# A delta-rule inverse on other PSUM banks, ScalarE's bank copies ahead of its exponentials, and query-key products between the levels

## The chip, the cores and the metric

The kernel runs on one core of a Trainium2 chip, as one launch. The metric is the device time of that launch in microseconds. A core has five engines with a queue each: TensorE (PE) multiplies matrices and writes into PSUM (8 banks of 512 fp32 columns on 128 partitions), VectorE (DVE), ScalarE (ACT) and GpSimd (POOL) work elementwise, and SyncE (SP) issues DMAs. Each queue runs in order; queues wait for each other by named counters (semaphores).

## What is computed

Two transformer blocks over 16 meta tokens and 256 tokens of 1024 features. The change touches the gated delta rule of the first block only (4 heads, chunks of 64 tokens):

```python
decay = jnp.cumsum(g.reshape(b, h, n, c), axis=-1)
diff = decay[..., :, None] - decay[..., None, :]
lmask = jnp.where(causal, jnp.exp(jnp.where(causal, diff, 0.0)), 0.0)
a = jnp.where(strict, jnp.einsum("bhnid,bhnjd->bhnij", k_beta, k) * lmask, 0.0)
m = a + jnp.eye(c, dtype=a.dtype)
u = lax.linalg.triangular_solve(m, v_beta, left_side=True, lower=True, unit_diagonal=True)
...
qk = jnp.where(causal, jnp.einsum("bhnid,bhnjd->bhnij", q, k) * lmask, 0.0)
...
v_new = uc - jnp.einsum("bhcd,bhde->bhce", wc, state)
o = jnp.einsum("bhcd,bhde->bhce", qd, state) + jnp.einsum("bhij,bhje->bhie", qkc, v_new)
```

`dn_z` (`zs` in the kernel) gates the output through a SiLU, and `sb_qkv`'s values (`sbv`) belong to the other attention branch of the same block.

## The kernel before

The program is written out by hand, engine by engine; nothing reorders it. The block's stages follow each other: normalisation and transposes; the input projection `x @ w_in` in units of 512 columns; the delta rule; gates, attention branch and output projection; the experts; then the whole second block.

**Projection.** Units 1 to 6 are split into a high and a low part, so that a result is three products. Each result takes the next of the banks 0 to 3 in turn (`group[0]`); before result n, `bank_free(n)` waits until ScalarE has copied out result n-4 (counter `proj_out` at n-3 or more). Results 0 to 19 are the feature groups, then come 20 and 21 (attention values of the two token tiles, `sbv`), 22 (values of the meta tokens), 23 and 24 (`zs` of the two tiles). Between them TensorE computes column sums of squares into `SSQ_BANK` (banks 2, 3, 6, 7; L835), and transposes of decay and beta rows (L845, L852) into banks 4, 6 and 7.

**ScalarE's order there.** First eight logarithms of the sums (L1655), then eight exponentials (L1658), three small exponentials for the decays (L1660 to L1662), three large ones of the decay masks (L1665, which wait for VectorE's L2128), and only then the copies of results 20, 21 and 22 and the two SiLUs of 23 and 24 (L1670).

**The inverse.** For 9 matrices (`PARTS`: two parts of four for the tiles, one with the meta tokens) the inverse of I + A is built on blocks that double in size, level 0 to 5, in both 64-row halves at once, and joined at the end. `AT` is the transposed A, `XIc` the inverse and `XITc` its transpose. A level is: TensorE forms A X (`AX_BANK`, L893); VectorE masks it into `TMc` (L2161); TensorE forms the products for both forms (`ROW_BANK` L904, `XAX_BANK` L908); VectorE subtracts them (L2171, L2172). Level 0 needs no second product: VectorE sets X to I minus the mask (L2166), and GpSimd makes the transpose of that from `AT` with a constant of its own (`level0T`; L660 and L663). The query-key products stand in banks 0 and 1; VectorE multiplies them by the decay masks into `QKT` (L2154), ahead of level 0, since `AX_BANK` takes the same banks. So TensorE's wait ahead of level 0 (L884) is for all eight steps of VectorE's counter `chunk_dve`.

**Counters:** `proj` results done, `proj_out` results copied out, `ssq_psum`/`ssq_ln` column sums and their logarithms, `row_psum` transposed rows, `decay_rows` the operands of the decay masks, `chunk_psum` and `chunk_dve` products and VectorE's steps ahead of the inverse, `inv_ax`, `inv_masked`, `inv_xax`, `inv_step` the steps of a level, `stacked` GpSimd's steps.

Of the kernel before, what the change touches and what calls it, by code (L numbers as in the profile page):

```python
# [13 lines left out]
ALU = mybir.AluOpType  # L14
# [3 lines left out]
P = 128  # L18
# [3 lines left out]
NT = SEQ // P  # L22
# [42 lines left out]
HALVES = ["eye2", "level0T"] + [f"level{i}" for i in range(LEVELS - 1)]  # L65
# [11 lines left out]
def shape_constants():  # L77
# [17 lines left out]
    put["level0T"] = (q % 2 == 1) & (row == q - 1)  # L95
# [16 lines left out]
def build(nc, t):  # L112
# [422 lines left out]
    AX_BANK = B[0], B[1], B[6][:, 0:HW]  # L535
    ROW_BANK = B[2], B[3], B[6][:, HW:2 * HW]
    XAX_BANK = B[4], B[5], B[6][:, 2 * HW:3 * HW]
# [80 lines left out]
    def _(pool):  # L618
# [36 lines left out]
        for i, part in enumerate(PARTS):  # L655
            n = part.stop - part.start
            pool.wait_ge(S("chunk_dve"), 4 + i)
            pool.wait_ge(S("stacked"), 2 * i + 2)
            for rs in HALF_ROWS:
                last = nc.gpsimd.tensor_tensor(XITc[rs, part, :], AT[rs, part, rs], halves("level0T", n)[rs], ALU.mult)  # L660
            last.then_inc(S("stacked"), 1)
            pool.wait_ge(S("stacked"), 2 * i + 3)
            nc.gpsimd.tensor_tensor(XITc[:, part, :], halves("eye2", n), XITc[:, part, :], ALU.subtract).then_inc(S("stacked"), 1)  # L663
# [21 lines left out]
    def _(pe):  # L685
# [198 lines left out]
        pe.wait_ge(S("chunk_dve"), 8)  # L884
        pe.wait_ge(S("chunk_act"), 3)
        for lv in range(INNER):
            for i, part in enumerate(level_parts(lv)):
                if lv:
                    pe.wait_ge(S("inv_step"), inverse_count(lv - 1, i))
# [7 lines left out]
            for i, part in enumerate(level_parts(lv)):  # L897
                pe.wait_ge(S("inv_masked"), inverse_count(lv, i))
                if lv == 1:
                    pe.wait_ge(S("stacked"), 2 * i + 4)  # L900
# [671 lines left out]
    def _(sc):  # L1572
# [79 lines left out]

        for c in range(8):
            sc.wait_ge(S("ssq_psum"), c + 1)
            act(sq[:, c, :], SSQ_BANK[c % 4][:, 0:L], ACT.Ln, bias=C("eps6")).then_inc(S("ssq_ln"), 1)  # L1655
        for c in range(8):
            sc.wait_ge(S("ssq_ln"), c + 1)
            act(sq[:, c, :], sq[:, c, :], ACT.Exp, scale=-0.5).then_inc(S("rnorm"), 1)  # L1658
        sc.wait_ge(S("dec_out"), 1)
# [7 lines left out]
        for n, (dst, r, f) in enumerate([(sbv[:, 0, :], P, ACT.Copy), (sbv[:, 1, :], P, ACT.Copy), (sbv[:, 2, 0:P], P, ACT.Copy),  # L1667
                                         (zs[:, 0, :], P, ACT.Silu), (zs[:, 1, :], P, ACT.Silu)]):
            sc.wait_ge(S("proj"), N_FM + n + 1)
            act(dst, B[(N_FM + n) % 4][0:r, 0:dst.shape[1]], f).then_inc(S("proj_out"), 1)  # L1670
# [323 lines left out]
    def _(dve):  # L1994
# [157 lines left out]
        for i in range(NT):  # L2152
            dve.wait_ge(S("chunk_psum"), i + 9)
# [668 lines left out]
```

## Time and profile before

| | us |
|---|---|
| median of 3 runs | 1001.61 |
| lowest and highest | 1001.59, 1003.16 |
| the profiled execution | 1003.22 |
| its span in the trace | 1001.4 |
| TensorE busy in the span | 939.9 |
| VectorE busy | 572.1 |
| ScalarE busy | 389.2 |
| GpSimd busy | 37.9 |

The profiled execution has 1.8 us outside its span and is 1.6 us above the median. In a timeline each row is a merged group of instructions: its start, the time from the first start to the last end, engine, line, operation, output and input tiles, shapes and count; the brackets give idle time of the engine just before and what ended it. An fp32 product shows as two matmul records, and ends of matmuls are modelled, so neighbouring groups overlap by a tenth of a microsecond. DVE is VectorE, ACT ScalarE, POOL GpSimd, SPq the queue that issues DMAs.

### The profile page before, as it was taken

Reading aid. Unit: us, or ns where it says so; the run is one execution under the profiler, and the core shown is the slowest. Engines: PE = TensorE matmul, PEld = TensorE weight load, DVE = VectorE, ACT = ScalarE, POOL = GpSimd, SP = SyncE. Lnnn points to the kernel's source line nnn. Section 1 sums busy time; section 2 is a strip of 40 time slices with the busy share of each in tenths; the row PEclk is TensorE's granted clock in tenths of the full one; section 3 lists DMA queues with packets and bytes.
Section 4 is the critical chain, followed back from the end, with each engine's and each line's share of the span. In section 5 each row is a group of like instructions: output and inputs, shape, how many; then the busy total and the mean of one; then the engine's idle time right before and its main releaser. Section 6 shows DMA issues by size and latency. Waiting matters only on the chain.

```text
span 1001.4 us, 14260 instructions
## 1 busy us (share of the span) xinstructions
PE 939.9 (94%) x5875; PEld 730.4 (73%) x5875; DVE 572.1 (57%) x903; ACT 389.2 (39%) x525; POOL 37.9 (4%) x59
## 2 busy tenths in 40 slices
PE   8999889999998999388889999999999999999997
PEld 7998786777775434142568888888888898888885
DVE  5886474995673102010086567665566786666564
ACT  4556403773251111010166455433433454433341
POOL 1410120002000000000000000000000000000000
PEclk9999999999999999798999999999999999999999
DMA  9843420446699999999987523554554444554421
GB/s 324 254 169 109 163 92 1 168 169 259 245 366 386 419 421 419 419 420 419 382 319 250 182 85 115 188 202 168 179 213 153 168 169 171 207 211 168 169 82 43
DMA packets 67563, 226.35 MB, mean 226 GB/s; under 512 B 4128, under 2 KB 5440, under 8 KB 55856
## 3 DMA queue, kind: packets, MB, share of 16 engines
q1 hardware_dynamic: 65648, 220.21, 58.2%
q0 software_dynamic: 1632, 5.26, 1.7%
q8 instruction: 41, 0.67, 0.3%
q14 instruction: 18, 0.15, 0.1%
q10 hardware_dynamic: 224, 0.07, 0.0%
HBM read 224.47 MB, written 1.05 MB: 225 GB/s over the span
## 4 chain that ended last, share of the span: by engine, by line
PE 76%; DMA 9%; DVE 9%; ACT 3%; issue 2%; SPq 1%; ACTq 0%; DVEq 0%
PE bank L1511 16%; PE bank L1500 11%; PE bank L1501 6%; PE bank L1217 5%; PE bank L762 5%; DMA arena<-in_expert_w_up 4%; PE bank L1365 4%; DMA ring<-in_expert_w_up 3%; PE bank L775 2%; PE bank L1085 2%; PE bank L1127 2%; PE bank L1427 2%; PE bank L1369 2%; PE bank L807 1%; PE bank L1355 1%
## 5 line engine op out<-in xcount | busy, mean ns | idle before, releaser
L2607 DVE TENSOR_TENSOR w_lo<-ring,w_hi 128x2048 fp32r<-128x2048 f32 x76 | 170.5, 2287 | 76.4 <-ACT w_hi L1853 76.2
L1853 ACT ACTIVATE w_hi<-ring 128x2048 fp32r<-128x2048 f32 x76 | 141.4, 1915 | 95.0 <-PE bank L1511 86.3
L1500 PE MATMUL bank<-xT_lo_hi,w_hi 128*128 128x512 f32 x480 | 170.0, 398 | 0.0
L1501 PE MATMUL bank<-xT_lo_hi,w_lo 128*128 128x256 f32 x480 | 134.8, 281 | 0.0
L1500 PEld LDWEIGHTS bank<-xT_lo_hi,w_hi 128*128 128x128 f32 x480 | 90.2, 188 | 22.3
L1511 PE MATMUL bank<-w_hi,hidden_hi 128*128 128x512 f32 x256 | 100.0, 391 | 0.0
L1511 PE MATMUL bank<-w_hi,hidden_lo 128*128 128x512 f32 x256 | 99.8, 390 | 0.0
L1511 PE MATMUL bank<-w_lo,hidden_hi 128*128 128x512 f32 x256 | 99.7, 389 | 0.0
L1501 PEld LDWEIGHTS bank<-xT_lo_hi,w_lo 128*128 128x128 f32 x480 | 90.7, 189 | 0.5
L1217 PE MATMUL bank<-ring,arena 128*32 128x512 f32 x256 | 52.5, 621 | 20.5 <-DMA arena<-in_expert_w_up 20.5
L1951 ACT ACTIVATE arena<-bank 128x256 f32<-128x256 f32 x64 | 21.1, 382 | 109.9 <-PE bank L1501 106.1
L1511 PEld LDWEIGHTS bank<-w_hi,hidden_lo 128*128 128x128 f32 x256 | 48.0, 188 | 10.4
L1511 PEld LDWEIGHTS bank<-w_hi,hidden_hi 128*128 128x128 f32 x256 | 48.0, 188 | 10.2
L1511 PEld LDWEIGHTS bank<-w_lo,hidden_hi 128*128 128x128 f32 x256 | 48.1, 188 | 9.7
L2499 DVE TENSOR_TENSOR X<-X,bank 128x256 f32<-128x256 f32 x9 | 3.8, 420 | 78.2 <-ACT X L1815 78.2
L2714 DVE TENSOR_TENSOR arena<-arena,bank 128x256 f32<-128x256 f32 x60 | 22.5, 417 | 44.6 <-ACT arena L1951 44.6
L2507 DVE COPY X<-bank 128x512 f32<-128x512 f32 x9 | 6.2, 692 | 68.8 <-PE bank L1255 61.1
L1217 PEld LDWEIGHTS bank<-ring,arena 128*32 128x32 f32 x256 | 13.9, 114 | 37.2 <-issue 37.2
L1217 PE MATMUL bank<-arena 128*32 128x512 f32 x160 | 38.3, 632 | 1.4 <-DMA ring<-in_expert_w_up 1.4
L1815 ACT ACTIVATE X<-bank 128x256 f32<-128x256 f32 x9 | 3.5, 384 | 88.6 <-PE bank L1217 88.6
L1365 PE MATMUL bank<-w_hi,xT_lo_hi 128*128 128x512 f32 x160 | 37.9, 389 | 0.0
L1277 PE MATMUL bank<-X 128*128 128x512 f32 x72 | 32.8, 598 | 2.7 <-DVE X L2507 2.7
(585 smaller groups left out, 1722.9 us busy)
## 6 DMA issues: line engine op xcount, KB each, us to landing
ring<-in_mlp_w_up SPq DMA_DIRECT2D x32, 1024.0 KB, 7.4
ring<-in_mlp_w_down SPq DMA_DIRECT2D x32, 1024.0 KB, 6.0
ring<-in_w_in SPq DMA_DIRECT2D x22, 1024.0 KB, 8.2
ring<-in_expert_w_gate SPq DMA_DIRECT2D x15, 1024.0 KB, 12.8
ring<-in_expert_w_up SPq DMA_DIRECT2D x15, 1024.0 KB, 15.5
ring<-in_expert_w_down SPq DMA_DIRECT2D x14, 1024.0 KB, 19.8
arena<-in_expert_w_down SPq DMA_DIRECT2D x12, 1024.0 KB, 22.4
ring<-in_attn_w_qkv SPq DMA_DIRECT2D x12, 1024.0 KB, 11.9
```

Of the source, the lines that this page charges most:

```text
L762: last = mm(B[n % 4][:, 0:L], w_[:, k * 512 + c * P:k * 512 + (c + 1) * P], x_[:, k, IN_0:IN_W], start=(p_ == 0 and k == 0), stop=(p_ == 2 ...
L775: last = mm(B[n % 4][0:r, :], x_[:, k, IN_0 + a:IN_0 + a + r], w_[:, k * 512:(k + 1) * 512], start=(p_ == 0 and k == 0), stop=(p_ == 2 and ...
L1217: last = mm(cube(B[4][CAP * e:CAP * (e + 1), :], 2), xs[:, k, (q % 2) * P + CAP * e:(q % 2) * P + CAP * (e + 1)], w_[e][:, :, k, :], start ...
L1277: last = mm(B[2 * i + half], hTs[:, (2 + i) * P:(3 + i) * P], ysb[:, half * 512:(half + 1) * 512], start=first, stop=final)
L1365: mm(bank, x_[:, k, i * P:(i + 1) * P], w_hi[:, k * 512:(k + 1) * 512], start=(k == 0 and x_ is xTH), stop=False)
L1500: mm(cube(B[4 + c], 2), w_hi[:, at], both_parts(k), start=(k == 0), stop=False)
L1501: last = mm(B[4 + c][:, 0:SEQ], w_lo[:, at], xTH[:, k, 0:SEQ], start=False, stop=(k == KD - 1))
L1511: last = mm(B[n], h_[:, j % 2, c, i * P:(i + 1) * P], w_[:, c * D + half * 512:c * D + (half + 1) * 512], start=(first and c == 0 and p_ = ...
L1853: act(whi[:, n % 2, half], slot(u)[:, half], ACT.Copy).then_inc(S("split_hi"), 1)
L1951: last = act(relu_t[:, pr, half], B[0][:, half] if (j, pr) == (0, 0) else B[4 + 2 * pr + cc][:, 0:SEQ], ACT.Copy)
L2607: tt(wlo[:, u % SLOTS, half], slot(u)[:, half], f32(whi[:, n % 2, half]), ALU.subtract).then_inc(S("split_lo"), 1)
L2714: last = tt(r_[:, cc, :], r_[:, cc, :], B[4 + 2 * pr + cc][:, SEQ:2 * SEQ], ALU.add)
```

## The change

Three edits of order and place, and one of work:

1. ScalarE copies out results 20 and 21 before the logarithms, and result 22 behind the eight exponentials. The SiLUs stay where they were.
2. The inverse uses other banks: `AX_BANK` and `ROW_BANK` are the halves of banks 4 and 6, `XAX_BANK` is banks 2 and 3, and the part with the meta tokens is in bank 7. Banks 0 and 1 keep the query-key products through the levels; VectorE multiplies them in levels 4 and 5, between its masks and its subtractions. TensorE waits ahead of level 0 for each part of `AT` by itself.
3. GpSimd no longer makes `XITc` of level 0; VectorE transposes `XIc` (in blocks of 32 x 32) ahead of level 1's masks. The constant `level0T` is gone, and TensorE's wait for GpSimd in level 1.

```diff
-    AX_BANK = B[0], B[1], B[6][:, 0:HW]
-    ROW_BANK = B[2], B[3], B[6][:, HW:2 * HW]
-    XAX_BANK = B[4], B[5], B[6][:, 2 * HW:3 * HW]
+    AX_BANK = B[4], B[6], B[7][:, 0:HW]
+    ROW_BANK = B[4][:, 4 * HW:8 * HW], B[6][:, 4 * HW:8 * HW], B[7][:, HW:2 * HW]
+    XAX_BANK = B[2], B[3], B[7][:, 2 * HW:3 * HW]
...
-        for i, part in enumerate(PARTS):
-            n = part.stop - part.start
-            pool.wait_ge(S("chunk_dve"), 4 + i)
-            pool.wait_ge(S("stacked"), 2 * i + 2)
-            for rs in HALF_ROWS:
-                last = nc.gpsimd.tensor_tensor(XITc[rs, part, :], AT[rs, part, rs], halves("level0T", n)[rs], ALU.mult)
-            last.then_inc(S("stacked"), 1)
-            pool.wait_ge(S("stacked"), 2 * i + 3)
-            nc.gpsimd.tensor_tensor(XITc[:, part, :], halves("eye2", n), XITc[:, part, :], ALU.subtract).then_inc(S("stacked"), 1)
...
-        pe.wait_ge(S("chunk_dve"), 8)
         pe.wait_ge(S("chunk_act"), 3)
         for lv in range(INNER):
             for i, part in enumerate(level_parts(lv)):
+                if lv == 0:
+                    pe.wait_ge(S("chunk_dve"), 4 + i)
...
-                if lv == 1:
-                    pe.wait_ge(S("stacked"), 2 * i + 4)
...
+        def tokens_out(n, dst, r, f=ACT.Copy):
+
+            sc.wait_ge(S("proj"), N_FM + n + 1)
+            act(dst, B[(N_FM + n) % 4][0:r, 0:dst.shape[1]], f).then_inc(S("proj_out"), 1)
+
+        for i in range(NT):
+            tokens_out(i, sbv[:, i, :], P)
         for c in range(8):
             sc.wait_ge(S("ssq_psum"), c + 1)
             act(sq[:, c, :], SSQ_BANK[c % 4][:, 0:L], ACT.Ln, bias=C("eps6")).then_inc(S("ssq_ln"), 1)
         for c in range(8):
             sc.wait_ge(S("ssq_ln"), c + 1)
             act(sq[:, c, :], sq[:, c, :], ACT.Exp, scale=-0.5).then_inc(S("rnorm"), 1)
+        tokens_out(2, sbv[:, 2, 0:P], P)
...
-        for n, (dst, r, f) in enumerate([(sbv[:, 0, :], P, ACT.Copy), (sbv[:, 1, :], P, ACT.Copy), (sbv[:, 2, 0:P], P, ACT.Copy),
-                                         (zs[:, 0, :], P, ACT.Silu), (zs[:, 1, :], P, ACT.Silu)]):
-            sc.wait_ge(S("proj"), N_FM + n + 1)
-            act(dst, B[(N_FM + n) % 4][0:r, 0:dst.shape[1]], f).then_inc(S("proj_out"), 1)
+        for i in range(NT):
+            tokens_out(3 + i, zs[:, i, :], P, ACT.Silu)
...
-        for i in range(NT):
-            dve.wait_ge(S("chunk_psum"), i + 9)
-            tt(flat(QKT[:, PARTS[i], :]), B[i], flat(LM[:, PARTS[i], :]), ALU.mult).then_inc(S("chunk_dve"), 1)
-
         dve.wait_ge(S("stacked"), 2)
         for lv in range(INNER):
+            if lv == 1:
+                for i, part in enumerate(PARTS):
+                    dve.wait_ge(S("inv_step"), inverse_count(0, i))
+                    nc.vector.transpose(flat(XITc[:, part, :]), flat(XIc[:, part, :]))
...
+            if lv >= META_LEVELS:
+                i = lv - META_LEVELS
+                dve.wait_ge(S("chunk_psum"), i + 9)
+                tt(flat(QKT[:, PARTS[i], :]), B[i], flat(LM[:, PARTS[i], :]), ALU.mult).then_inc(S("chunk_dve"), 1)
```

What stands on ScalarE from the column sums to the SiLUs; first before (L1655 logarithms, L1658 and L1660 to L1662 exponentials, L1665 the decay masks, L1670 the copies and SiLUs; `arena` holds all these tiles):

```order
L1655 ACT_TABLE_LOAD
L1655 ACTIVATE arena<-bank,cst 128x272 [waits ssq_psum] x8
L1658 ACT_TABLE_LOAD
L1658 ACTIVATE arena<-arena 128x272 [waits ssq_ln] x8
L1660 ACTIVATE small<-small 128x9 [waits dec_out]
...
L1665 ACTIVATE arena<-arena 128x512 [waits decay_rows] x2
L1665 ACTIVATE arena<-arena 128x128 [waits decay_rows]
L1670 ACTIVATE arena<-bank 128x512 [waits proj] x2
L1670 ACTIVATE arena<-bank 128x128 [waits proj]
L1670 ACT_TABLE_LOAD
L1670 ACTIVATE arena<-bank 128x512 [waits proj] x2
```

The same place on ScalarE in the changed kernel (L1645 copies and SiLUs, L1651 logarithms, L1654 to L1659 exponentials, L1662 the decay masks):

```order
L1645 ACTIVATE arena<-bank 128x512 [waits proj] x2
L1651 ACT_TABLE_LOAD
L1651 ACTIVATE arena<-bank,cst 128x272 [waits ssq_psum] x8
L1654 ACT_TABLE_LOAD
L1654 ACTIVATE arena<-arena 128x272 [waits ssq_ln] x8
L1645 ACTIVATE arena<-bank 128x128 [waits proj]
L1657 ACTIVATE small<-small 128x9 [waits dec_out]
...
L1662 ACTIVATE arena<-arena 128x512 [waits decay_rows] x2
L1662 ACTIVATE arena<-arena 128x128 [waits decay_rows]
L1645 ACT_TABLE_LOAD
L1645 ACTIVATE arena<-bank 128x512 [waits proj] x2
```

The two 512-column copies have moved from behind the decay masks to ahead of the logarithms' table load, and the 128-column copy to behind the exponentials.

VectorE around level 0, before (L2151 makes `AT`, L2154 `QKT`, L2161 the masks, L2166 X of level 0, L2171 and L2172 the subtractions of level 1):

```order
L2151 TENSOR_TENSOR arena<-bank,arena 128x128 [waits chunk_psum]
L2154 TENSOR_TENSOR arena<-bank,arena 128x512 [waits chunk_psum] x2
L2161 TENSOR_TENSOR arena<-bank,cst 128x256 [waits inv_ax,stacked]
L2161 TENSOR_TENSOR arena<-bank,cst 128x256 [waits inv_ax]
L2161 TENSOR_TENSOR arena<-bank,cst 128x64 [waits inv_ax]
L2166 TENSOR_TENSOR arena<-cst,arena 128x256 [waits inv_masked] x2
L2166 TENSOR_TENSOR arena<-cst,arena 128x64 [waits inv_masked]
L2161 TENSOR_TENSOR arena<-bank,cst 128x256 [waits inv_ax] x2
L2161 TENSOR_TENSOR arena<-bank,cst 128x64 [waits inv_ax]
```

VectorE at the same place in the changed kernel (L2146 `AT`, L2156 masks, L2165 X of level 0, L2152 the transposes):

```order
L2146 TENSOR_TENSOR arena<-bank,arena 128x128 [waits chunk_psum]
L2156 TENSOR_TENSOR arena<-bank,cst 128x256 [waits inv_ax,stacked]
L2156 TENSOR_TENSOR arena<-bank,cst 128x256 [waits inv_ax]
L2156 TENSOR_TENSOR arena<-bank,cst 128x64 [waits inv_ax]
L2165 TENSOR_TENSOR arena<-cst,arena 128x256 [waits inv_masked] x2
L2165 TENSOR_TENSOR arena<-cst,arena 128x64 [waits inv_masked]
L2152 STREAM_TRANSPOSE arena<-arena 128x256 [waits inv_step] x2
L2152 STREAM_TRANSPOSE arena<-arena 128x64 [waits inv_step]
L2156 TENSOR_TENSOR arena<-bank,cst 128x256 [waits inv_ax] x2
L2156 TENSOR_TENSOR arena<-bank,cst 128x64 [waits inv_ax]
```

The two products of 512 columns have left the place ahead of the first mask, and three transposes have come in between level 0's X and level 1's masks.

VectorE in level 4 of the changed kernel (L2160 is the moved `QKT` product, L2170 and L2171 the subtractions):

```order
L2156 TENSOR_TENSOR arena<-bank,cst 128x256 [waits inv_ax] x2
L2160 TENSOR_TENSOR arena<-bank,arena 128x512 [waits chunk_psum]
L2170 TENSOR_TENSOR arena<-arena,bank 128x256 [waits inv_step,inv_xax,inv_masked]
L2171 TENSOR_TENSOR arena<-arena,bank 128x256
L2170 TENSOR_TENSOR arena<-arena,bank 128x256 [waits inv_step,inv_xax,inv_masked]
```

One 512-column product stands between the second mask and the first subtraction; level 5 has the other.

## Rows read from the trace of the kernel before

**Rows 1.** The page: the chain that ended last, and the DMA slices.

```profile
PE 76%; DMA 9%; DVE 9%; ACT 3%; issue 2%; SPq 1%; ACTq 0%; DVEq 0%
...
DMA  9843420446699999999987523554554444554421
```

**Rows 2.** Who waited for whom on TensorE: us in total, times, longest.

```profile
PE bank L775 <- ACT arena L1670: 3.2, 1, 3.2
```

**Rows 3.** Timeline of TensorE, from result 23 to the rows of beta.

```profile
101.22 2.11 PE L775 MATMUL bank<-first_hi,in_hi 128*128 128x512 f32 x8
...
106.80 1.14 PE L845 MATMUL bank<-cst,arena 128*128 128x128 f32 x9
111.16 2.49 PE L775 MATMUL bank<-first_hi,in_hi 128*128 128x512 f32 x8 [3.22 <-ACT arena L1670]
113.45 3.21 PE L775 MATMUL bank<-first_hi,in_lo 128*128 128x512 f32 x8
...
118.32 1.15 PE L852 MATMUL bank<-cst,arena 128*128 128x128 f32 x9
```

**Rows 4.** Busy time by stretch: span, PE, PEld, DVE, ACT, POOL, clock, DMA, GB/s.

```profile
111.20:116.50 5.30, 5.30 (x17) 4.18 (x17) 0.00 (x0) 2.35 (x4) 0.00 (x0) 0.68 0.00 0
...
126.50:149.10 22.60, 20.48 (x580) 18.98 (x580) 16.11 (x47) 2.17 (x6) 4.91 (x10) 1.00 0.28 96
...
509.00:510.00 1.00, 1.00 (x7) 1.00 (x6) 1.00 (x1) 0.00 (x0) 0.00 (x0) 0.50 0.99 379
```

**Rows 5.** Timeline of TensorE's small products and column sums (L835), then of ScalarE.

```profile
92.72 0.28 PE L824 MATMUL bank<-small,cst 128*128 128x8 f32 x2
...
93.78 3.88 PE L835 MATMUL bank<-arena,cst 128*128 128x272 f32 x16
...
94.50 3.69 ACT L1655 ACTIVATE arena<-bank,cst 128x272 f32<-128x272 f32 x8 [7.15 <-PE bank L835]
98.21 1.28 ACT L1658 ACT_TABLE_LOAD   x1
...
110.44 1.23 ACT L1670 ACTIVATE arena<-bank 128x512 f32<-128x512 f32 x3
...
118.52 0.60 ACT L1670 ACTIVATE arena<-bank 128x512 f32<-128x512 f32 x1 [4.93 <-PE bank L775]
```

**Rows 6.** Timeline of VectorE: the operands of the decay masks.

```profile
107.51 2.42 DVE L2128 TENSOR_SCALAR arena<-bank,small 128x128 f32<-128x128 f32 x9 [4.64 <-PE bank L845]
```

**Rows 7.** Timeline of TensorE and VectorE up to level 0.

```profile
123.73 1.95 PE L881 MATMUL bank<-arena 128*128 128x128 f32 x16
126.54 1.26 PE L893 MATMUL bank<-cst,arena 64*64 64x64 f32 x36 [0.86 <-DVE arena L2154]
...
125.20 1.28 DVE L2154 TENSOR_TENSOR arena<-bank,arena 128x512 f32<-128x512 f32 x2
```

**Rows 8.** Timeline of VectorE, GpSimd and TensorE from level 0 to 1.

```profile
128.21 0.42 DVE L2166 TENSOR_TENSOR arena<-cst,arena 128x256 f32<-128x256 f32 x1
...
128.54 0.95 DVE L2166 TENSOR_TENSOR arena<-cst,arena 128x256 f32<-128x256 f32 x1
...
129.41 0.31 DVE L2166 TENSOR_TENSOR arena<-cst,arena 128x64 f32<-128x64 f32 x1
129.64 0.41 DVE L2161 TENSOR_TENSOR arena<-bank,cst 128x256 f32<-128x256 f32 x1
...
128.25 0.96 POOL L663 TENSOR_TENSOR arena<-cst,arena 128x256 f32<-128x256 f32 x1
...
130.17 0.63 PE L904 MATMUL bank<-arena 64*64 64x64 f32 x16
```

**Rows 9.** Timeline of VectorE in level 5: last mask, first subtraction.

```profile
144.58 0.42 DVE L2161 TENSOR_TENSOR arena<-bank,cst 128x256 f32<-128x256 f32 x1 [0.45 <-PE bank L893]
145.57 0.42 DVE L2171 TENSOR_TENSOR arena<-arena,bank 128x256 f32<-128x256 f32 x1 [0.56 <-PE bank L908]
```

**Rows 10.** What SyncE's queue waited for, first of its rows.

```profile
SPq L575 <- PE bank L1085: 26.4, 2, 17.2
```

More of the change, by code:

```diff
@@ L64 @@
 VECTORS = ["emb_g", "emb_b", "mix0", "mix1", "mlp0", "mlp1", "ln2_g", "ln2_b", "ln1_g", "ln1_b"]
-HALVES = ["eye2", "level0T"] + [f"level{i}" for i in range(LEVELS - 1)]
+HALVES = ["eye2"] + [f"level{i}" for i in range(LEVELS - 1)]
 SMALL = {"hmask": DN_H, "idx4": NG, "desc4": NG, "desc8": NE, "freq": HALF, "eps5": 1, "eps5a": 1, "eps6": 1, "one": 1, "zero": 1, "fold": 8}
@@ L94, in shape_constants @@
     put["eye2"] = row == q
-    put["level0T"] = (q % 2 == 1) & (row == q - 1)
     for i in range(LEVELS - 1):
```

## The prediction

> **What bounds the kernel now.** I read the chain that ended last first: TensorE is 76% of it, DMA 9% [rows 1]. So time saved on TensorE's path is time saved, unless a later stage is held by something that didn't move with it. Then I read TensorE's list of waits for those that end on an engine the change touches. One stands out: a single wait of 3.2 us of the L775 products on ScalarE's L1670 [rows 2]. The timeline shows where: the transposes L845 start at 106.80, and result 24 starts at 111.16 only, after 3.22 us of idle time [rows 3]. `bank_free(24)` wants result 20 copied out of bank 0, and that copy is the first of the three at 110.44 [rows 5]. ScalarE had been stuck behind the decay masks, whose operands VectorE makes in 107.51 to 109.93 [rows 6]. The wait has a tail: the windows show a granted clock of 0.68 in 111.20 to 116.50 with TensorE busy all through, that is a mix of 1.2 and 2.4 GHz, where the stretch before had been at full clock and then idle [rows 4]; a group of eight products takes 3.21 us in it [rows 3].
>
> **Part 1, the copies moved ahead.** Result 21, the later of the two, is finished when the small products start at 92.72 [rows 5]; the two copies (0.60 us each, the price of L1670's 512 columns [rows 5]) would thus be done at about 93.5. ScalarE sat idle there for 7.15 us [rows 5], so that time covers them. What is queued behind the new wait on ScalarE is the table load and the eight logarithms. A load is 1.28 us [rows 5]: 93.5 + 1.3 = 94.8, against a first logarithm at 94.50 now, 0.3 late at most. Who waits for it: the fifth column sum needs the first logarithm. TensorE's eight sums take 3.81 us from 93.78, 0.48 each, so the fifth starts at 95.7; the first logarithm ends at 94.8 + 0.46 = 95.3 (3.69 / 8 [rows 5]). Covered with 0.4 to spare; without that cover each tenth would count in full. The 128-column copy goes behind the exponentials, 0.3 us into a gap that lasts until 108.
>
> So result 24 follows L845 at once. L845 takes about 0.98 us to the next start, which gives 107.78 in place of 111.16: 3.38 us. Its three passes then run like those of result 23, 101.22 to 106.80, 5.58 us, in place of 111.16 to 118.32, 7.16 us: 1.58 us more from the clock [rows 3]. **Sum of part 1: 4.96 us**; L852 starts at 113.36.
>
> What is late next? L852 wants the decay operands, done at 109.93 [rows 6]: 3.4 us of slack. L860 wants both SiLUs; the last ran 118.52 to 119.12, right behind result 24 [rows 5], and it moves along, with its table already loaded once the decay masks are done. VectorE's products wait for L852. All of these hang on result 24 and shift by the same amount. GpSimd's parameter DMAs now start behind `memset` rather than at 130.3, beside a weight load which nobody needs before 180; I price that at nothing, with up to 0.2 us if the VectorE steps beside it suffer.
>
> **Part 2, level 0 earlier.** TensorE ends L881 at 125.68 and starts level 0 at 126.54, waiting 0.86 us for VectorE's L2154 [rows 7]. That product goes away there, `AT` has been ready since about 125.3, when VectorE went on to L2154, and the row names no other engine. **Gain 0.86 us.**
>
> **Part 3, the transpose on VectorE.** Now the second L2166 takes 0.95 us where the first, of the same form, takes 0.42; it starts at 128.54, and GpSimd's L663 stands beside it from 128.25 for 0.96 [rows 8]. Without GpSimd, three L2166 take 0.33 + 0.33 (128.21 to 128.54, twice) + 0.13 from 128.21 (a 64-column step: between a quarter of 0.33 and the 0.23 from 129.41 to 129.64 beside GpSimd), and the next instruction would start at 129.00 in place of 129.64: 0.64 us gained. Then come the transposes, which the trace of before doesn't contain. Bounds: below, half of a `tensor_tensor`'s spacing, 0.4 us for the three, as they have one input where it has two; above, the slowest row of 256 columns, 0.95 each [rows 8], 2.1 us in all. I take the spacing of the other 256-column steps, 0.34 + 0.34 + 0.13 = 0.81 us, since columns, type and engine are the same. VectorE then reaches level 1's mask 0.17 us later than now, counted from level 0's start, and TensorE's L904 (130.17, 0.1 behind the mask's end at 130.05 [rows 8]) follows it. **Cost 0.17 us** (bounds: gain of 0.24, loss of 1.5).
> The Trainium skill (SBUF — State Buffer, "Who interferes with whom") says that a VectorE instruction with two SBUF inputs contends with a GpSimd instruction that reads SBUF, and the 0.95 against 0.42 agrees. The Trainium skill (Vector Engine (DVE) Microarchitecture Reference, section 3.8) says that the transpose mode sustains one element per cycle per lane; no run here shows it yet, and by it the middle value would hold.
>
> **Part 4, the moved products.** In level 5 VectorE's last mask starts at 144.58 and its first subtraction at 145.57 [rows 9]; level 4 looks alike. Mask 0.34 + product 0.60 (about half of L2154's 1.28 for two [rows 7]) end at 145.52. It fits, with 0.05 us over. What hides them is TensorE's L904 and L908; without it each would cost 0.6. I take 0, at most 0.2. The banks are no term: TensorE and VectorE take turns by the same counters as before. The constant's missing 64 columns cost nothing.
>
> **Sum.** 4.96 + 0.86 - 0.17 = 5.65, say 5.7 us. The profiled execution of 1003.22 would be 997.5. It lies 1.6 above the median of 1001.61; the same difference from the median gives **995.9 us**.
>
> **Does it last to the end?** From slice 15 on the DMA engines are at 9 tenths for eight slices [rows 1]; there, bytes set the pace. But the loads before and at its start are issued on a TensorE release (the longest row of that kind: SyncE's L575 behind L1085, 26.4 us in two waits [rows 10]), and none of these stands earlier than the change. So the whole saturated stretch starts 5.7 us earlier.
>
> **Rivals.**
> *Smaller gain:* the transposes cost their upper bound, 1.3 us more than taken: 997.2. Or ScalarE's table load holds the logarithms up for twice its 1.28 us: first logarithm 96.0 to 96.5, fifth sum 0.8 late, result 22 0.7 late: 996.6. Both: 997.9. For it: no row shows a transpose. Against: behind the eight logarithms (ending 98.19) the load starts at 98.21 and is done at 99.49 [rows 5], with nothing more. 0.13.
> The Trainium skill (ScalarE: Activation LUTs, "What ACT_TABLE_LOAD costs") puts a drain of about 1.38 us beside the 1.28 of the load, which speaks against putting work ahead of a load; this case's trace shows no such drain.
> *Clock elsewhere:* the dip behind a wait depends on when it comes. At 509.00 the clock is 0.50 in a busy stretch [rows 4]; if a shift of 5.7 us makes that dip vanish, or makes another as long, it is some 1.6 us (the price of part 1's dip): 994.3 or 997.5. 0.09.
> *Nothing comes out:* the gain is taken back, because the expert weights arrive when they did before, or the wait of result 24 goes over to something unseen right behind it: 1001.6 to 1000.9. Rows 10 speak against the first, rows 6 against the second. 0.05.
> *Slower:* the clock falls over the inverse. Between level 0 and level 1 TensorE has nothing but waits if the transposes are slow, and the 64-column products that follow don't bring the clock back. At low clock a group of eight takes 3.21 in place of 1.98 [rows 3], 1.62 times; on 20.48 us of busy time in 126.50 to 149.10 [rows 4] that is 12.7 us, net 7 us slower: 1008.6. It decides from 9.2 us of low-clock busy time on. Against it: the same stretch ran at 1.00 behind an idle gap of 0.86 us [rows 4, 7], and that gap goes. 0.03.
> The forecast has the remaining 0.70.
>
> **The numbers.** Range: below, 995.9 less the cheap transposes (0.4) and a vanished dip (1.6), 993.9; above, 997.9; the runs of before spread over 1.6, so I round outwards to 993.5 and 998.5. Less than 0.2% (2 us) can't be told from no change in this kernel. Faster by more: 0.70 + 0.13 + 0.09 = 0.92; within: 0.05; slower: 0.03.
>
> **What would show it.** TensorE's wait on the bank copy is gone and result 24 starts about 1 us behind L845 (else part 1 is wrong); the granted clock is 1.00 from 105 to 125; result 24 takes 5.6 us. The idle time before level 0 is under 0.1 us. Three transposes of about 0.4, 0.4 and 0.2 us, no L2165 above 0.45; first subtraction in levels 4 and 5 still released by TensorE. The inverse's own length, from level 0's start to its last product, grows by 0.2 us. The distance between the start of the attention products and the end of the span is unchanged within 1.5 us; if it grew by 5, the rival without gain is right. The prediction is most wrong if the loads of the expert stage don't move.

## The result, and the profile after

| | us |
|---|---|
| before, median (4 runs) | 1001.6 |
| changed, median (4 runs, 994.41 to 998.08) | 995.95 |
| ratio, with its 95% interval | 0.9943 [0.9927, 0.9959] |
| profiled execution, changed | 998.08 |
| its span | 996.0 (before: 1001.4) |

The forecast was 995.9. A second comparison gave 0.9933 [0.9911, 0.9954]. Over all comparisons the kernel before ran from 998.74 to 1006.84 us, so a single run says little about a change of 5.7 us; the steps have to be read in the trace. Three runs far above all others (1073 us of the interleaved kernel, 1078 and 3336 of the kernel before) are in no ratio and in no such span.

TensorE's timeline of the changed kernel (start, length, line, operation, tiles, count; in brackets the idle time before and what ended it). Lines have moved by ten or so: L835 is the old L845, L765 the old L775, L842 the old L852, L884 the old L893, L893 the old L904, L680 the old L690 (a helper whose products nobody reads; its first ones here follow the inverse):

```profile
106.76 1.14 PE L835 MATMUL bank<-cst,arena 128*128 128x128 f32 x9
107.66 2.09 PE L765 MATMUL bank<-first_hi,in_hi 128*128 128x512 f32 x8
...
113.23 1.15 PE L842 MATMUL bank<-cst,arena 128*128 128x128 f32 x9
...
120.53 1.26 PE L884 MATMUL bank<-cst,arena 64*64 64x64 f32 x36
...
124.25 0.68 PE L893 MATMUL bank<-arena 64*64 64x64 f32 x16 [0.32 <-DVE arena L2156]
...
143.14 0.80 PE L680 MATMUL bank<-cst 128*128 128x128 f32 x4
```

Against [rows 3]: result 24 follows L835 0.90 us after its start, where it was 4.36, with no idle time in brackets; and it takes 5.57 us to L842's start, where it took 7.16. Against [rows 7]: no idle time before level 0. Against [rows 8]: 3.72 us from level 0's start to the first row product, where it was 3.63.

ScalarE's timeline, at the logarithms:

```profile
92.87 0.60 ACT L1645 ACTIVATE arena<-bank 128x512 f32<-128x512 f32 x1 [4.84 <-PE bank L765]
93.49 1.28 ACT L1651 ACT_TABLE_LOAD   x1
94.78 3.36 ACT L1651 ACTIVATE arena<-bank,cst 128x272 f32<-128x272 f32 x8
```

The copy ends at 93.47, the load starts at 93.49, the first logarithm at 94.78, 0.28 later than in [rows 5]; the eight end at 98.14 against 98.19, since the first ones now find their sums waiting.

VectorE's timeline, level 0 to 1 and level 4 (L2165 X of level 0, L2152 the transposes, L2156 masks, L2160 the moved product, L2170 first subtraction):

```profile
122.19 0.89 DVE L2165 TENSOR_TENSOR arena<-cst,arena 128x256 f32<-128x256 f32 x3
123.00 0.89 DVE L2152 STREAM_TRANSPOSE arena<-arena 128x256 f32<-128x256 f32 x3
123.81 0.85 DVE L2156 TENSOR_TENSOR arena<-bank,cst 128x256 f32<-128x256 f32 x3
...
135.15 0.42 DVE L2156 TENSOR_TENSOR arena<-bank,cst 128x256 f32<-128x256 f32 x1 [0.32 <-PE bank L884]
135.49 0.68 DVE L2160 TENSOR_TENSOR arena<-bank,arena 128x512 f32<-128x512 f32 x1
136.14 0.42 DVE L2170 TENSOR_TENSOR arena<-arena,bank 128x256 f32<-128x256 f32 x1
```

Three X tiles take 0.81 us to the next start (before, beside GpSimd, 1.43: 128.21 to 129.64 in [rows 8]), and the three transposes 0.81 as well.

The kernel before, at the end of the inverse:

```profile
149.11 0.71 PE L690 MATMUL bank<-cst 128*128 128x128 f32 x4
```

Counted there (149.11 us before, 143.14 here) the change is 5.97 us ahead. Some of that is lost behind it and some comes back, and the busy table says part of why. Columns: span, busy time of PE, PEld, DVE, ACT, POOL, granted clock, DMA share, GB/s. First the changed kernel:

```profile
143.00:147.00 4.00, 4.00 (x21) 2.13 (x19) 1.62 (x3) 0.28 (x1) 0.00 (x0) 0.58 0.00 0
276.00:281.00 5.00, 5.00 (x27) 4.52 (x27) 4.14 (x24) 5.00 (x6) 0.00 (x0) 0.66 1.03 429
...
112.00:117.00 5.00, 4.81 (x38) 4.29 (x37) 2.99 (x8) 3.97 (x9) 2.56 (x4) 1.00 0.48 145
```

and the changed kernel's second trace in two of the same stretches:

```profile
143.00:147.00 4.00, 3.75 (x104) 3.41 (x104) 2.76 (x8) 0.64 (x2) 0.00 (x0) 1.00 0.02 4
276.00:281.00 5.00, 5.00 (x47) 4.85 (x45) 4.45 (x14) 3.41 (x6) 0.00 (x0) 1.00 0.81 282
```

The first table's low clock at 112 to 117 is gone as forecast, but this execution has two others, at 143 and at 276, in work that the change didn't touch. Its second trace, in the second table, has neither. The trace of the kernel before had a dip of its own at 509 [rows 4], which isn't in the changed trace.

Further on, TensorE's timeline at two places in the expert stage and behind it, first before, then changed (L1253 is the old L1264, L1354 the old L1365):

```profile
366.51 3.70 PE L1264 MATMUL bank<-arena,X 128*128 128x512 f32 x8 [0.69 <-ACT X L1825]
...
508.04 3.19 PE L697 MATMUL bank<-cst,X 128*128 128x128 f32 x16 [2.66 <-DVE X L2026]
...
522.54 3.79 PE L1365 MATMUL bank<-w_hi,xT_lo_hi 128*128 128x512 f32 x16
```

```profile
362.74 3.70 PE L1253 MATMUL bank<-arena,X 128*128 128x512 f32 x8 [0.69 <-ACT X L1820]
...
516.83 3.79 PE L1354 MATMUL bank<-w_hi,xT_lo_hi 128*128 128x512 f32 x16
```

The lead is 3.77 us at the first place and 5.71 at the second, so 1.94 us of the pair's difference come from this stretch, which the change doesn't touch. It takes 156.03 us in the first trace of the kernel before and 151.9 to 154.1 in all thirteen others, the second trace of the kernel before (152.2) among them.

### The profile page after: what moved, and what is told of

Read it like the earlier page. It is cut to its first block, busy times and chain, and to the rows that moved or that the text cites. A ratio compares the mean times of both kernels' runs of the same rounds, so it can differ in the third digit from the quotient of the medians.

```text
span 996.0 us, 14248 instructions
## 1 busy us (share of the span) xinstructions
PE 941.0 (94%) x5875; PEld 730.5 (73%) x5875; DVE 571.9 (57%) x906; ACT 388.9 (39%) x525; POOL 32.6 (3%) x50
## 4 chain that ended last, share of the span: by engine, by line
PE 80%; DVE 8%; DMA 7%; ACT 2%; issue 2%; SPq 0%; ACTq 0%; DVEq 0%
PE bank L1500 16%; PE bank L1489 11%; PE bank L1490 6%; PE bank L1206 5%; PE bank L752 5%; DMA arena<-in_expert_w_up 4%; PE bank L1354 4%; PE bank L1074 2%; PE bank L765 2%; PE bank L1116 2%; PE bank L1416 2%; DMA ring<-in_expert_w_up 2%; PE bank L1358 2%; PE bank L1169 2%; PE bank L797 1%
## 5 line engine op out<-in xcount | busy, mean ns | idle before, releaser
L1354 PE MATMUL bank<-w_hi,xT_lo_hi 128*128 128x512 f32 x160 | 38.0, 390 | 0.0
```

Source lines behind the costliest of these rows:

```text
L1354: mm(bank, x_[:, k, i * P:(i + 1) * P], w_hi[:, k * 512:(k + 1) * 512], start=(k == 0 and x_ is xTH), stop=False)
```

## Experiments

All are variants of one of the two kernels. They ran in three comparisons, in which the median of the kernel before was 1002.5 us (changed again, copies only, inverse only, wait filled), 1001.37 (before again, products first, copies late, interleaved) and 1002.24 (the other four), so across them the ratios are to be compared. "Level 0 to rows" is the time from level 0's start to level 1's first row product.

| kernel | median us | ratio to before, interval |
|---|---|---|
| changed, again | 995.7 | 0.9933 [0.9911, 0.9954] |
| copies only | 997.07 | 0.9944 [0.9923, 0.9965] |
| inverse only | 999.68 | 0.9972 [0.9956, 0.9989] |
| inverse only, again | 1000.05 | 0.9983 [0.997, 0.9996] |
| before, wait filled | 999.71 | 0.9974 [0.9959, 0.9989] |
| before, again | 1001.71 | 1.0009 [0.9994, 1.0025] |
| products first | 995.19 | 0.9936 [0.9917, 0.9956] |
| copies late | 995.75 | 0.9944 [0.9922, 0.9966] |
| transposed twice | 996.67 | 0.995 [0.9934, 0.9965] |
| GpSimd transposes | 996.16 | 0.9942 [0.9924, 0.9959] |
| interleaved | 994.44 | 0.9924 [0.9904, 0.9944] |
| interleaved, filled | 994.88 | 0.9928 [0.9913, 0.9942] |

### The copies alone

```diff
 (the kernel before)
+        for i in range(NT):
+            tokens_out(i, sbv[:, i, :], P)
         for c in range(8):
             sc.wait_ge(S("ssq_psum"), c + 1)
...
+        tokens_out(2, sbv[:, 2, 0:P], P)
         sc.wait_ge(S("dec_out"), 1)
...
+        for i in range(NT):
+            tokens_out(3 + i, zs[:, i, :], P, ACT.Silu)
```

> The kernel before with ScalarE's copies moved ahead and nothing else. Theory: this carries nearly all: 1001.6 - 5.0 = 996.6 us, ratio 0.995; in the trace L852's transposes start 5.0 us earlier (113.3), level 0 at 121.5, the idle time before level 0 stays 0.9. Rival (the gain comes from the inverse): ratio 0.999 or more.

TensorE's timeline:

```profile
107.54 2.09 PE L775 MATMUL bank<-first_hi,in_hi 128*128 128x512 f32 x8
...
113.11 1.15 PE L852 MATMUL bank<-cst,arena 128*128 128x128 f32 x9
...
121.33 1.26 PE L893 MATMUL bank<-cst,arena 64*64 64x64 f32 x36 [0.86 <-DVE arena L2160]
...
124.96 0.63 PE L904 MATMUL bank<-arena 64*64 64x64 f32 x16
```

L852 starts at 113.11 and level 0 at 121.33 with its 0.86 us of idle time and 3.63 us from level 0 to rows, all as in the kernel before but 5.2 us earlier (0.16 of it was there ahead of result 24). From rows to the end of the inverse it takes 19.54 us, where the kernel before takes 18.94; 0.44 of that is one gap on TensorE in level 2 for which the trace names no cause. By the medians of its comparison (1002.5, 997.07, and 995.7 for the changed kernel) this one edit carries 5.4 of 6.8 us, and the rival is out.

### The inverse alone

```diff
 (the changed kernel)
-        for i in range(NT):
-            tokens_out(i, sbv[:, i, :], P)
...
-        tokens_out(2, sbv[:, 2, 0:P], P)
...
-        for i in range(NT):
-            tokens_out(3 + i, zs[:, i, :], P, ACT.Silu)
+        (the loop over all five, as before)
```

> The changed kernel with ScalarE's copies put back behind the decay masks, so banks, products between the levels and VectorE's transposes alone. Theory: 0.7 to 0.8 us, 1000.8 us, ratio 0.9992, which the timing alone can't tell from 1; in the trace the wait for result 20's copy is back with 3.2 us, level 0 starts 0.9 us earlier than in the kernel before (125.6), and level 1's first row product 0.8 us earlier (129.35). Rival (the inverse gains more than that): below 0.998.

TensorE's timeline:

```profile
110.62 2.06 PE L765 MATMUL bank<-first_hi,in_hi 128*128 128x512 f32 x8 [3.21 <-ACT arena L1659]
...
116.16 1.15 PE L842 MATMUL bank<-cst,arena 128*128 128x128 f32 x9
...
123.45 1.26 PE L884 MATMUL bank<-cst,arena 64*64 64x64 f32 x36
```

The wait is back with 3.21 us. But result 24 takes 5.54 us behind it, and the busy table (columns as above) has the clock at its full level there, 1.00:

```profile
111.00:114.00 3.00, 3.00 (x15) 2.48 (x14) 0.00 (x0) 2.02 (x3) 0.00 (x0) 1.00 0.00 0
```

That is why level 0 starts at 123.45, not at the expected 125.6. From L842 to level 0 it is 7.29 us, where it was 8.22 [rows 3, 7]: 0.93 gained, as expected. The median, 2.8 us below that of before, asked for the next run.

> The inverse-only kernel once more. Its first comparison gave 2.8 us (interval 1.1 to 4.4) where the sum of its parts is 0.8, and its trace had no low clock anywhere in a busy stretch before the experts. Theory: that was partly a lucky draw; with more runs it comes to 0.8 to 2 us, 1000.3 us, and this trace shows the low clock behind the 3.2 us wait (result 24 takes 7.2 us) or elsewhere. Rival (without the 0.86 us of idle time ahead of level 0 the clock no longer falls in this stage): again no dip before 270 us, and 999.7 us or less.

TensorE's timeline, and the same stretch of the busy table:

```profile
110.76 2.90 PE L765 MATMUL bank<-first_hi,in_hi 128*128 128x512 f32 x8 [3.21 <-ACT arena L1659]
...
117.91 1.15 PE L842 MATMUL bank<-cst,arena 128*128 128x128 f32 x9
```

```profile
111.00:114.00 3.00, 3.00 (x10) 2.35 (x10) 0.00 (x0) 2.15 (x4) 0.00 (x0) 0.62 0.00 0
```

Same program, and now the clock is 0.62 there and result 24 takes 7.15 us. So whether the tail follows the wait differs from one execution to the next. The interval now takes in the sum's 0.9992. By the ratios, both comparisons still lie below it, by 2.0 and 0.9 us, and what that is stays open (below).

### The wait, filled

```diff
 (the kernel before)
             last.then_inc(S("row_psum"), 1)
+        keep_going(4, 5)
         split_tokens(6, [xblk(1)])
```

> The kernel before with four fp32 products of 512 columns into bank 5 (nobody reads them) just before result 24, about 3.4 us, so TensorE is busy while it waits for ScalarE's copy. Theory: the wait (3.4 us) and the low clock behind it (1.6 us) are two terms, and this removes only the second: result 24 starts at about 111.3 as before but takes 5.6 us in place of 7.2, clock 1.00 in 111 to 116.5, time 1001.6 - 1.5 = 1000.1 us, ratio 0.9985. Rival (the clock falls for another reason than the idle time): result 24 takes 7.2 us again, and the time is 1001.6 or a little above.

TensorE's timeline (L690 is the filling):

```profile
107.69 3.60 PE L690 MATMUL bank<-cst 128*128 128x512 f32 x8
111.07 2.09 PE L775 MATMUL bank<-first_hi,in_hi 128*128 128x512 f32 x8
...
116.62 1.15 PE L853 MATMUL bank<-cst,arena 128*128 128x128 f32 x9
...
126.98 2.20 PE L894 MATMUL bank<-arena 64*64 64x64 f32 x36 [0.88 <-DVE arena L2167]
```

Result 24 starts as late as before and takes 5.55 us. So the wait of 3.4 us and the clock of 1.6 us are two terms: the first stands here without the second. That busy work in the wait removes the second isn't shown by this one trace, since the inverse-only kernel had one without the tail as well; two things speak for it. The ratio's interval has the kernel 1.1 to 4.1 us faster than before, and none of the nine traces of kernels with the copies ahead, in which TensorE is busy there too, has a low clock at this place. The same trace shows the clock falling later, in level 1, where the products of L894 take 2.20 us, not 1.26; from level 0 to the end of the inverse it takes 25.10 us, where the first trace of the kernel before takes 22.57.

### The kernel before, again

> The kernel before itself, for a second trace. The trace of the inverse-only kernel had the 3.2 us wait and no low clock behind it, so theory: whether the clock falls behind that wait differs from execution to execution; this trace has the wait of 3.2 us before result 24 again, and result 24 takes 5.6 or 7.2 us, with nothing in the program different. With the dip and without, the time should differ by 1.6 us. Rival: the kernel before always has the dip (7.2 us) and the inverse-only kernel had lost it by something in the change.

The trace, TensorE's timeline and one stretch of the busy table:

```profile
111.43 3.21 PE L775 MATMUL bank<-first_hi,in_hi 128*128 128x512 f32 x8 [3.22 <-ACT arena L1670]
...
118.58 1.15 PE L852 MATMUL bank<-cst,arena 128*128 128x128 f32 x9
...
151.31 0.71 PE L690 MATMUL bank<-cst 128*128 128x128 f32 x4
...
129.00:133.00 4.00, 4.00 (x82) 3.92 (x84) 2.06 (x6) 0.00 (x0) 2.95 (x7) 0.57 0.24 82
```

The dip behind the wait is there (7.15 us), and a second one in level 1, which the first trace didn't have: from L852 to L690 it is 32.73 us here and 30.79 there, so it costs 1.9. The rival, that the kernel before always has the first dip, isn't refuted by this trace, but it needs another cause in the inverse-only kernel, whose second trace has the dip.

### The changed kernel, again

> The changed kernel once more, beside the parts of it. My theory: 995.9 us, ratio to before 0.9943, result 24 starting at 107.7 and level 0 at 120.5 in the trace as before. What may differ is where the granted clock dips: the first trace of the changed kernel has dips in busy stretches at 143 to 147 and 276 to 281 us and none at 503 to 507, the kernel before has one at 508 to 512 and none at the other two. Theory: these dips are not tied to the change, so this second trace has them at other places, and the span moves with them by 1 to 2 us. Rival: they are tied to the new order (the shorter inverse), so the second trace shows them at 143 and 276 again.

The second trace starts result 24 at 107.82 and level 0 at 120.69, and shows no low clock in a busy stretch before the expert stage (table above). So the new order doesn't bring the dips at 143 and 276 each time. That it has nothing to do with them isn't shown, and over all fourteen traces they don't fall just anywhere: a dip at 274 to 281 us is in six of the nine traces of kernels with the copies ahead and in none of the five others, and the one at 143 to 147 comes back in the kernel with the copies behind the exponentials. The one at 276 costs the profiled pair 0.8 us.

### The products ahead of level 0

```diff
 (the changed kernel)
+        for i in range(NT):
+            dve.wait_ge(S("chunk_psum"), i + 9)
+            tt(flat(QKT[:, PARTS[i], :]), B[i], flat(LM[:, PARTS[i], :]), ALU.mult).then_inc(S("chunk_dve"), 1)
         dve.wait_ge(S("stacked"), 2)
...
-            if lv >= META_LEVELS:
-                ...
```

> The changed kernel with the two query-key products put back ahead of level 0, new banks kept. Theory: the idle time before level 0 is back with 0.86 us and everything behind starts 0.9 us later: 995.8 + 0.9 = 996.7 us; the first subtraction of levels 4 and 5 starts at the same distance from its mask as in the changed kernel, since the products were hidden there. Rival (the products in levels 4 and 5 cost what they saved): 995.8 again, with levels 4 and 5 each 0.4 us shorter than in the changed kernel.

TensorE, then VectorE (L2149 the products, L2159 masks):

```profile
118.78 1.95 PE L871 MATMUL bank<-arena 128*128 128x128 f32 x16
120.65 1.27 PE L884 MATMUL bank<-cst,arena 64*64 64x64 f32 x36
...
120.25 1.28 DVE L2149 TENSOR_TENSOR arena<-bank,arena 128x512 f32<-128x512 f32 x2
121.45 0.95 DVE L2159 TENSOR_TENSOR arena<-bank,cst 128x256 f32<-128x256 f32 x3
...
136.26 0.42 DVE L2169 TENSOR_TENSOR arena<-arena,bank 128x256 f32<-128x256 f32 x1 [0.57 <-PE bank L897]
```

My expectation was wrong. TensorE starts level 0 right behind L871 although the products stand ahead of the masks: with `AX_BANK` in other banks, and with a wait for each part of `AT`, nothing of level 0 depends on them. VectorE is done with them when the first mask's operand arrives (121.45 is 0.80 behind level 0's start, as without them). From the first row product to L680 it is 18.88 us, in the changed kernel 18.89. The 0.9 us come from the banks and the finer wait together; neither was run alone, and by the order of the program each needs the other. Where the products stand is worth nothing, ahead of level 0 or between the levels.

### The copies behind the exponentials

```diff
 (the changed kernel)
-        for i in range(NT):
-            tokens_out(i, sbv[:, i, :], P)
         for c in range(8):
             sc.wait_ge(S("ssq_psum"), c + 1)
...
+        for i in range(NT):
+            tokens_out(i, sbv[:, i, :], P)
         tokens_out(2, sbv[:, 2, 0:P], P)
```

> The changed kernel with all three copies behind the eight exponentials of the norms, none ahead of the logarithms. Result 24 wants its bank at 107.8 us and the copies would be done by 103.5, so theory: same time as the changed kernel, 995.8 us, no wait before result 24, and the first logarithm back at 94.5 from 94.78. Rival (it matters that the banks are free early, or that the decay exponentials come right behind the others): 996.5 or more.

ScalarE's timeline, then TensorE's:

```profile
101.88 1.22 ACT L1645 ACTIVATE arena<-bank 128x512 f32<-128x512 f32 x3
...
107.50 2.09 PE L765 MATMUL bank<-first_hi,in_hi 128*128 128x512 f32 x8
```

All three copies are done at 103.1, result 24 starts as early as ever, and the time is the same. Ahead of the decay masks, either place for the copies will do.

### The transposes: twice, by GpSimd, interleaved

```diff
 (the changed kernel)
                     nc.vector.transpose(flat(XITc[:, part, :]), flat(XIc[:, part, :]))
+                beside = TM.rearrange("p c i -> p (c i)")[:, NM * HW:2 * NM * HW]
+                for i, part in enumerate(PARTS):
+                    nc.vector.transpose(beside[:, part.start * HW:part.stop * HW], flat(XIc[:, part, :]))
```

> The changed kernel with three more transposes of the same tiles in the same place, into a tile that nobody reads: the suspected cost doubled. Theory: in the changed kernel's trace the three are 0.81 us from the first's start to the next instruction, and all of it is on TensorE's path; so level 1's first row product starts 0.8 us later, counted from level 0's start (4.5 in place of 3.72), and so does all behind: 996.6 us. Rival (TensorE waits there for its own product anyway, part of the transposes is hidden): 0.4 or less.

TensorE's timeline:

```profile
124.95 0.68 PE L893 MATMUL bank<-arena 64*64 64x64 f32 x16 [1.10 <-DVE arena L2159]
```

Level 0 starts at 120.45 there: 4.50 us to rows, 0.78 more than with one set. All of the transposes' time is on the path.

The GpSimd kernel:

```diff
 (the changed kernel)
+        for i, part in enumerate(PARTS):
+            ...
+            for rs in HALF_ROWS:
+                last = nc.gpsimd.tensor_tensor(XITc[rs, part, :], AT[rs, part, rs], halves("level0T", n)[rs], ALU.mult)
+            ...
+            nc.gpsimd.tensor_tensor(XITc[:, part, :], halves("eye2", n), XITc[:, part, :], ALU.subtract).then_inc(S("stacked"), 1)
...
+                if lv == 1:
+                    pe.wait_ge(S("stacked"), 2 * i + 4)
...
-            if lv == 1:
-                for i, part in enumerate(PARTS):
-                    dve.wait_ge(S("inv_step"), inverse_count(0, i))
-                    nc.vector.transpose(flat(XITc[:, part, :]), flat(XIc[:, part, :]))
```

> The changed kernel with GpSimd making the level 0 transpose as before, and no transpose on VectorE. Theory: moving it to VectorE brought nothing by itself: 0.8 us of transposes against 0.64 us of contention. So the second subtraction of level 0 takes 0.95 us again beside GpSimd, and level 1's first row product starts at 3.63 us from level 0's start in place of 3.72: 995.7 us. Rival (level 0 now starts so early that GpSimd isn't ready): TensorE's wait in level 1 is released by GpSimd, and the level ends 0.5 us or more later: 996.3.

VectorE, TensorE, then GpSimd:

```profile
122.77 1.93 DVE L2173 TENSOR_TENSOR arena<-cst,arena 128x256 f32<-128x256 f32 x3
...
125.08 0.68 PE L905 MATMUL bank<-arena 64*64 64x64 f32 x16
...
123.82 0.79 POOL L663 TENSOR_TENSOR arena<-cst,arena 128x256 f32<-128x256 f32 x1
```

Level 0 starts at 121.10: 3.98 us to rows, 0.26 worse than VectorE's transposes and 0.35 worse than expected. The three X tiles take 1.93 us beside GpSimd, where they took 0.89 alone. Neither theory nor rival had that: TensorE is released by VectorE, not by GpSimd, but with level 0 earlier VectorE meets more of GpSimd's work. Behind the rows this trace takes 0.66 us more to the end of the inverse than the changed kernel's (19.55 and 18.89); 0.60 of it is one gap on TensorE in level 4 with no cause named, like that of the copies-only kernel, and it isn't counted here.
The Trainium skill (SBUF — State Buffer, "Who interferes with whom") has two-input VectorE instructions contend with GpSimd ones that read SBUF, and this agrees.

```diff
 (interleaved: the changed kernel; the loop of three transposes ahead of level 1 goes)
             for i, part in enumerate(level_parts(lv)):
                 n = part.stop - part.start
+                if lv == 1:
+                    dve.wait_ge(S("inv_step"), inverse_count(0, i))
+                    nc.vector.transpose(flat(XITc[:, part, :]), flat(XIc[:, part, :]))
                 dve.wait_ge(S("inv_ax"), inverse_count(lv, i))
```

> The changed kernel with each of VectorE's three transposes right ahead of the level 1 mask of its own part, instead of all three ahead of the first mask. The first mask waits only for the first transpose: the row products of level 1 should start 0.4 us earlier counted from level 0's start (3.3 us in place of 3.72), since TensorE then sits idle 0.32 us less. Theory: 995.8 - 0.3 to 0.4 = 995.4 us, visible in the trace, not in the timing. Rival (TensorE is then held by the second part's mask, or by its own queue): level 1 ends when it did, no gain in the start of level 2.

VectorE's first transpose, then TensorE:

```profile
123.01 0.44 DVE L2153 STREAM_TRANSPOSE arena<-arena 128x256 f32<-128x256 f32 x1
...
123.88 0.68 PE L893 MATMUL bank<-arena 64*64 64x64 f32 x16
```

Level 0 starts at 120.53 as in the changed kernel, the row products at 123.88 instead of 124.25, and L680 at 142.76 instead of 143.14: 0.38 us, kept to the end of the inverse. It has the lowest median of all; the timing alone doesn't separate it from the changed kernel.

```diff
 (the interleaved kernel)
             if lv == 0:
+                keep_going(2, 5, 2 * P)
                 continue
```

> The interleaved kernel with two fp32 products of 256 columns into bank 5 (nobody reads them) between level 0 and level 1, where TensorE is idle for 0.87 us. Theory: the low clock at 143 to 147 us, seen in two of four traces of kernels with the change, follows the stretch of short products with gaps, and filling the largest gap makes it rarer: 994.4 us, none of the trace's dips before 270 us, times closer together. Rival (the filling doesn't fit the gap): level 1 starts up to 0.2 us later, 994.6 to 995.0.

TensorE's timeline (L680 is the filling):

```profile
121.66 1.13 PE L680 MATMUL bank<-cst 128*128 128x256 f32 x4
...
123.93 0.68 PE L894 MATMUL bank<-arena 64*64 64x64 f32 x16
```

The filling costs 0.11 us (level 0 at 120.47, so 3.46 to rows against 3.35), its trace has no dip in a busy stretch before 270, nor has the interleaved kernel's; both have one at 274 to 278. One trace each decides nothing on how often dips come; the time is the same.

## Why the prediction was right

**Part 1, the copies.** Forecast 4.96 us: 3.38 for the wait and 1.58 for the clock. Measured in the profiled pair: 3.46 and 1.59. The copies-only kernel shows the term by itself (result 24 right behind L845, 5.57 us long), and the filled wait shows the first part standing without the second. The cover for ScalarE's new place held: the first logarithm started 0.28 us late and nobody waited. The rival in which the table load holds the logarithms up for twice its 1.28 us is out: the copy ends at 93.47, the load starts at 93.49, the first logarithm at 94.78. The Trainium skill (ScalarE: Activation LUTs, "What ACT_TABLE_LOAD costs") has a drain of about 1.38 us beside each load; these rows differ from that, and they decide. The 1.58 us for the clock, which I took as certain, come in part by luck, though: of four traces with the wait left empty, three have the low clock and one doesn't.

**Part 2, 0.86 us.** Measured 0.92 (8.22 to 7.30 from L852 or L842 to level 0). The size was right, the reason half right. I put the gain down to the product that leaves the place ahead of level 0; the products-first kernel shows that it needn't leave. The finer wait and the free banks do it, together.

**Part 3, the transpose.** Forecast a cost of 0.17, measured 0.09. The transposes took 0.44, 0.40 and 0.20 us and 0.81 to the next instruction, as taken. The comparison was too kind to GpSimd's way, which stood at its old time. At the new time GpSimd's way takes 3.98 us from level 0 to rows and VectorE's 3.72, so VectorE's gains 0.26.
The Trainium skill (Vector Engine (DVE) Microarchitecture Reference, section 3.8) gives one element per cycle per lane; 192 columns more take 0.20 to 0.24 us here, 1.0 to 1.2 ns each, in line with that.

**Part 4, nothing.** Right: with the products first or between the levels, the rest of the inverse takes 18.9 us. The room was as small as said: in level 4 the subtraction at 136.14 starts when the product lets it, while in the products-first kernel it waits 0.57 us for TensorE and starts at the same distance (0.99 us) from its mask. I had named "still released by TensorE" as the sign; that sign failed without cost.

**To the end.** 5.97 us at the end of the inverse, 5.4 in the span, 5.65 in the medians. How the profiled pair got from 5.97 to 5.4 is in part luck. "Clock elsewhere" came true in it: a dip of 1.45 us at 143 (from L680 to the attention's first products 20.19 us; 18.74 in the traces without it) and one of 0.8 at 276 brought the lead down to 3.8 us at L1264, at 366; then the stretch up to 522 gave 1.9 back, with the one dip less at 509 in it. The distance from the attention's first products to the end is 0.9 us shorter than before (832.7 and 833.5), within the 1.5 that I had named. The rival "nothing comes out" fell, and the better evidence is in the second trace: it is at the start of that stretch at 360.68, 5.8 us ahead of the first trace of the kernel before and 8.0 ahead of the second, and needs 153.2 us for it, where those two need 156.0 and 152.2. So at most 1 us of the lead is taken back there. That the median hit to 0.1 is more than the method can promise: the changed kernel's runs lie 3.7 us apart.

**What stays open.** By the ratios the inverse-only kernel is 1.7 and 2.8 us faster than before in its two comparisons, against a sum of 0.8. In the traces, a dip in level 1 shows up in two of the four that have idle time ahead of level 0 (before again, and filled wait) and in none of the ten that don't. That would be a gain of the change that I didn't count, of 1.9 to 2.5 us times its frequency, but four traces are too few to call it shown. Against it may stand the dip at 276, which only kernels with the copies ahead have shown. And why the stretch from 366 to 522 takes 151.9 us in one trace and 156.0 in another wasn't looked into; in the longest, TensorE also stands idle for 2.66 us ahead of 508, with the dip right behind.

## What to carry to other kernels

When an engine waits in order for something late, look at what stands behind it that another engine wants for a trifle, here a bank copy of 0.6 us: moving it ahead of the wait saves the wait, and often the low clock behind it. If a buffer's reader holds up the next stage, another bank with a wait for exactly what is needed does more than moving the reader. And price a contention or an overlap at the time at which it will happen after the change, not where it stands now.

## What the runs showed of the hardware

Behind the same idle time of 3.2 us, TensorE's granted clock fell in three traces of four (a result of 7.15 us, not 5.55); the inverse-only kernel alone showed both, 1.00 and 0.62 at 111 to 114 us. In the one trace in which TensorE was kept busy through that time it didn't fall.

Dips to about half clock also come in stretches where TensorE has work all through, behind idle times of no more than 0.9 us, in one execution of a kernel and not in the next: at 127 to 133 us, 143 to 147 and 274 to 281. They cost 1.9 and 2.5 us (before again and filled wait, in level 1), 1.45 and 0.8 us (changed, at 143 and 276). They come back at the same few places. The dip at 508 to 512 in the kernel before isn't of this kind: it stands behind 2.66 us of idle time. With the stretch from 366 to 522 us, whose length differs by up to 4 us, they are what these traces show of why runs of one kernel differ by several us; two single traces should be compared stage by stage, with the clock of each stage beside it.

VectorE's three X tiles, two inputs in SBUF each, took 1.93 us beside GpSimd's work on SBUF (the GpSimd kernel) and 0.89 alone (the changed kernel).
